# Where the inverse root of the RMS norms is made in a two-layer encoder trunk: sums land on all partitions by a tile of ones, logarithm and exponential in place of root, reciprocal and spread

## The chip, the core and the metric

One core of a Trainium2 chip runs the whole program. The metric is the device time in microseconds (us). The engines are called as in the profile: PE is TensorE (matmuls; PEld its weight loads), ACT is ScalarE, DVE is VectorE, POOL is GpSimd, and SP issues most DMAs.

## What is computed

A trunk of two layers on 512 tokens of width 1024, in float32. Each mixer and each feed-forward part stands between two RMS norms (from the reference):

```python
def rms_norm(x, g):
    y = xf * lax.rsqrt(jnp.mean(xf * xf, axis=-1, keepdims=True) + RMS_EPS) * g
for layer in range(DEPTH):
    h = rms_norm(x, norm_mix_pre[layer])
    m = even_mixer(h, ...) if layer % 2 == 0 else odd_mixer(h, positions, ...)
    x = x + rms_norm(m, norm_mix_post[layer])
    h = rms_norm(x, norm_ffn_pre[layer])
    f = conv_ffn(h, ...)
    x = x + rms_norm(f, norm_ffn_post[layer])
```

The even mixer is a gated linear recurrence beside stick-breaking attention, the odd one a sliding-window attention with rotary positions and sinks. The feed-forward part projects up to 2 x 2816, convolves over three tokens, gates, and projects down.

## The kernel before

**Layout.** Activations lie with the 1024 channels on partitions (8 tiles of 128) and the 512 tokens along the free axis, so a norm's sum runs over partitions. Each product of two float32 matrices is made of three matmuls (`three`, L1649): both factors are split into a high part, rounded to float32r, and a low part, the difference. ACT makes high parts (`split_hi`, L702; hx_hi), DVE low parts (`split_lo`, L1099; hx_lo). Weights come in units of 1 MB into a ring of three slots, loaded by SP.

**Norms before a matmul phase** (pre-norms p = 0 to 3). The gain is folded into hx_hi and hx_lo; the inverse root of a token, which is the same for all channels, is multiplied in when a result is taken out of PSUM, from the tile `rbc` (128 x 512, the same row on all partitions). ACT squares (`square`, L709), POOL (DVE for p = 0) adds up to `sumsq`. PE then makes token sums in columns (`mean_square`, L1705): for each 128 tokens a matmul with `sumsq` stationary and one column of ones moving. ACT takes the root (`root`, L717) into `std` (128 x 4), DVE the reciprocal `rcol` and four scaled identities `diag` (`inverse_rms`, L1120). PE multiplies `ones` with `diag`, which spreads the row over all partitions (`spread`, L1741), and DVE copies it to `rbc` (L1140). `rcol` itself is used as a column for the values of both attentions (L1287, L1042).

**Norms behind a phase** (boundaries bi = 0, 1, 2: the first mixer, the first feed-forward part, the second mixer). They go by token halves h = 0, 1, so that PE can begin with the next phase's half 0 while half 1 is being normed. `post_mean_square` (L1714) has one-column matmuls again, for two groups of tokens; in half 1 the last square is not added to `sumsq` but is a second source, which doubles them. `post_root` (L737), `post_inverse` (L1131) and `post_spread` (L1731) follow; the result stays in PSUM, in bank 6 or 7, left half. DVE then walks over the channel tiles (`boundary`, L1409): `normed` (L1421) the product into the right half of the bank, `add` (L1427) to x, `lo` (L1431) hx_lo, and ACT `hi` (L922) between. The last norm of all is made in another layout and has no part in this.

**Order.** Each engine has one queue, written out by hand; waits are semaphores. PE's places for the norm's matmuls are fixed steps in the stream of the projection: the sum of half 0 at step 4 and its spread at step 6 of the half 1 output (L1981 to L1986), those of half 1 at k = 5 and 7 of the next phase's first unit (`first_units`, L2011), the pre-norm's sum and spread as hooks within its third unit (L2034, L2037). `first_units` takes half 0 of two units, then half 1, each k behind `hx_ready`. In the second boundary ACT's queue is `raw(0)`, `root(2)`, then `raw(1)`; `raw` (L908) copies a query or key tile for the rotary, whose halves SP swaps by DMA (L550), 8 issues per tile, before DVE's products (`rope_finish`, L1548) and PE's first scores (`sw_scores`, L2117).

ACT needs the right function table. `preload_act_table_set` loads one ahead of its use; where a function is not in the loaded set, the compiler puts a load in front of it.

Of the kernel before, what the change touches and what calls it, by code (L numbers as in the profile page):

```python
# [21 lines left out]
P = 128  # L22
T = 512
# [129 lines left out]
def build(nc, io, out):  # L153
# [76 lines left out]
    diag = at("diag", [P, TT, P], F32, tmp0 + T * 4)  # L230
# [144 lines left out]

    def gate_bank(g):

        return bank(g % 3)
# [3 lines left out]
    def sb_set(h):  # L382
# [18 lines left out]
    sq_done, sum_done, ms_mm, std_done, rcol_done, diag_done, bc_mm, rbc_done = (sem(n) for n in (  # L401
        "sq_done", "sum_done", "ms_mm", "std_done", "rcol_done", "diag_done", "bc_mm", "rbc_done"))
    psq_done, psum_done, pms_mm, pstd_done, prcol_done, pdiag_done, pbc_mm = (sem(n) for n in (
        "psq_done", "psum_done", "pms_mm", "pstd_done", "prcol_done", "pdiag_done", "pbc_mm"))
# [231 lines left out]
    def _(pool):  # L636
# [12 lines left out]
        def whole_sums(bi, n):  # L649

            for i in range(1, n):
                pool.wait_ge(psq_done, post_squares(bi) + i + 1)
                if i == 1:
                    pool.wait_ge(ms_mm, bi + 1)
# [46 lines left out]
    def _(act):  # L701
# [52 lines left out]
        act.preload_act_table_set("sqrt_and_others")  # L754
# [17 lines left out]
        root(0)  # L772
# [145 lines left out]
        def boundary(bi, which, layer, last, splits):  # L918
# [6 lines left out]
            if bi == 1:  # L925
                act.preload_act_table_set("sqrt_and_others")
# [4 lines left out]
            post_root(bi, 0)  # L931
# [10 lines left out]
            post_root(bi, 1)  # L942
# [7 lines left out]
            root(bi + 1)  # L950

        def out_projection(layer):

            u = U_OUT[layer]
            act.preload_act_table_set("sqrt_and_others")
# [83 lines left out]
        act.wait_ge(unit_done, U_V + 1)  # L1039
        for t in range(TT):  # L1040
# [57 lines left out]
    def _(dve):  # L1098
# [21 lines left out]
        def inverse_rms(p):  # L1120

            dve.wait_ge(std_done, p + 1)
            if p:
                dve.wait_ge(pdiag_done, 2 * p)
            dve.reciprocal(rcol[:], std[:]).then_inc(rcol_done, 1)
            dve.wait_ge(rcol_done, p + 1)
            for t in range(TT):
                ins = dve.tensor_scalar(diag[:, t, :], ident, rcol[:, t:t + 1], None, ALU.mult)
            ins.then_inc(diag_done, 1)

        def post_inverse(bi, h):  # L1131

            dve.wait_ge(pstd_done, 2 * bi + h + 1)
            dve.reciprocal(rcol[:, 2 * h:2 * h + 2], std[:, 2 * h:2 * h + 2]).then_inc(prcol_done, 1)
            dve.wait_ge(prcol_done, 2 * bi + h + 1)
            for t in (2 * h, 2 * h + 1):
                ins = dve.tensor_scalar(diag[:, t, :], ident, rcol[:, t:t + 1], None, ALU.mult)
            ins.then_inc(pdiag_done, 1)

        def spread(p):  # L1140
            dve.wait_ge(bc_mm, p + 1)
            dve.tensor_copy(rbc[:], bank(6 if p else 4)).then_inc(rbc_done, 1)

# [48 lines left out]
        inverse_rms(0)  # L1192
        spread(0)
# [133 lines left out]
        for n in range(4):  # L1327
            evac(n)
        softplus_lambda()
        split_lo(3)  # L1330
        evac(4)
# [77 lines left out]
        def boundary(bi, post, pre, last, splits):  # L1409
# [238 lines left out]
    def _(pe):  # L1648
# [56 lines left out]
        def mean_square(p):  # L1705

            if p:
                pe.wait_ge(pstd_done, 2 * p)
            pe.wait_ge(sum_done, pre_sums(p + 1))
            for t in range(TT):  # L1710
                last = pe.matmul(bank(7)[:, t:t + 1], sumsq[:, P * t:P * t + P], ones[:, 0:1], start=t == 0, stop=t == TT - 1)
            last.then_inc(ms_mm, 1)

        def post_mean_square(bi, h):  # L1714

            if h:
                pe.wait_ge(pstd_done, 2 * bi + 1)
            else:
                pe.wait_ge(std_done, bi + 1)
# [3 lines left out]
            q = last_square(bi, h)  # L1723
            for t in (2 * h, 2 * h + 1):
                c = P * (t - 2 * h)
                srcs = (sumsq[:, P * t:P * t + P], sq[q % 3][:, HALF + c:HALF + c + P])[0:h + 1]
                for i, src in enumerate(srcs):
                    last = pe.matmul(bank(7)[:, t:t + 1], src, ones[:, 0:1], start=i == 0 and t == 2 * h, stop=i == h and t == 2 * h + 1)
            last.then_inc(pms_mm, 1)

# [577 lines left out]
```

## Time and profile before

| | us |
|---|---|
| median of 3 runs | 1085.07 (1084.81 to 1085.59) |
| the profiled execution | 1085.26 |
| its span, first to last instruction | 1083.5 |
| PE busy | 1074.3 |
| DVE busy | 688.2 |
| ACT busy | 478.2 |
| POOL busy | 59.2 |

### The profile page before, as it was taken

The page shows a single profiled execution, that of the slowest core. Times are in us where ns is not written, and L with a number is a line of the kernel's source. Part 1 is how long each engine was busy: PE and PEld are TensorE (multiplying, and loading weights), DVE is VectorE, ACT ScalarE, POOL GpSimd, SP SyncE. Part 2 cuts the span into 40 slices and gives each one's busy share as a digit, 9 for nine tenths or more (in the row PEclk, how much of TensorE's full clock was granted, in tenths as well). Part 3 has the DMA queues.
Part 4 walks back from the last instruction along what each step waited for, and adds up shares of the span by engine and source line. Part 5 has one row for each costly group of instructions (what it writes and reads, how often), then busy time and mean ns, then how long its engine had stood idle before and what let it go on. Part 6 is the DMA issues. An engine that isn't in the chain of part 4 may idle for free.

```text
span 1083.5 us, 14799 instructions
## 1 busy us (share of the span) xinstructions
PE 1074.3 (99%) x5860; PEld 906.6 (84%) x5860; DVE 688.2 (64%) x925; ACT 478.2 (44%) x691; POOL 59.2 (5%) x55
## 2 busy tenths in 40 slices
PE   9999999999999999999999999999999999999997
PEld 7876889988888888888899877998888888888886
DVE  6784975878767676522257877397867667751323
ACT  6455764645444444312235477464534343432321
POOL 0000002310000000001103000230000000000000
PEclk9999999999999999999999999999999999999999
DMA  7332141122222222232232513312323232321322
GB/s 237 117 117 75 45 153 67 52 79 106 90 103 90 96 97 93 92 107 82 94 118 68 181 59 117 117 40 79 117 78 116 77 116 77 117 78 61 114 97 77
DMA packets 23206, 105.61 MB, mean 97 GB/s; under 512 B 4080, under 2 KB 6896, under 8 KB 12528
## 3 DMA queue, kind: packets, MB, share of 16 engines
q1 hardware_dynamic: 23008, 104.84, 27.9%
q8 instruction: 39, 0.64, 0.2%
q14 instruction: 15, 0.12, 0.0%
q10 hardware_dynamic: 144, 0.01, 0.0%
HBM read 98.15 MB, written 2.10 MB: 93 GB/s over the span
## 4 chain that ended last, share of the span: by engine, by line
PE 93%; DVE 3%; ACT 2%; DMA 1%; issue 1%; SPq 0%; DVEq 0%
PE ps L1651 29%; PE ps L1653 29%; PE ps L1652 29%; PE ps L1835 1%; PE ps L1861 1%; PE ps L1846 1%; DVE ps L1421 1%; PE ps L2132 1%; DVE x L1427 1%; PE ps L2143 1%; DVE hx_lo L1431 1%; PE ps L2159 1%; ACT w_hi_s L707 1%; ACT prob L1056 0%; DVE w_lo_s L1103 0%
## 5 line engine op out<-in xcount | busy, mean ns | idle before, releaser
L1651 PE MATMUL ps<-hx_hi,w_hi 128*128 128x512 f32 x812 | 320.5, 395 | 0.3 <-DVE w_lo L1150 0.3
L1653 PE MATMUL ps<-hx_hi,w_lo 128*128 128x512 f32 x812 | 316.3, 390 | 0.0
L1652 PE MATMUL ps<-hx_lo,w_hi 128*128 128x512 f32 x812 | 316.2, 389 | 0.0
L1103 DVE TENSOR_TENSOR w_lo<-w_raw,w_hi 128x2048 fp32r<-128x2048 f32 (+1 forms) x74 | 167.6, 2265 | 119.5 <-ACT w_hi L707 119.4
L707 ACT ACTIVATE w_hi<-w_raw 128x2048 fp32r<-128x2048 f32 (+1 forms) x76 | 142.2, 1870 | 106.5 <-DMA w_raw<-in_ffn_w_down 90.8
L1651 PEld LDWEIGHTS ps<-hx_hi,w_hi 128*128 128x128 f32 x812 | 152.4, 188 | 37.7 <-issue 6.8
L1653 PEld LDWEIGHTS ps<-hx_hi,w_lo 128*128 128x128 f32 x812 | 152.4, 188 | 31.8
L1652 PEld LDWEIGHTS ps<-hx_lo,w_hi 128*128 128x128 f32 x812 | 152.5, 188 | 31.0 <-issue 0.5
L965 ACT ACTIVATE cg<-ug,vec 128x512 f32<-128x512 f32 x44 | 35.9, 816 | 140.8 <-DVE ug L1467 140.8
L1476 DVE SCALAR_TENSOR_TENSOR cg<-ug,vec,cg 128x511 f32<-128x511 f32 x88 | 65.8, 747 | 20.4 <-ACT cg L965 20.4
L977 ACT ACTIVATE g_hi<-cv 128x512 f32 (+1 forms) x44 | 27.8, 632 | 111.1 <-DVE cv L1485 111.1
L1467 DVE TENSOR_TENSOR ug<-ps,rbc 128x512 f32<-128x512 f32 x44 | 30.3, 690 | 61.4 <-PE ps L1653 61.4
L1651 PE MATMUL ps<-w_hi,g_hi 128*128 128x512 f32 x176 | 68.8, 391 | 0.0
L1653 PE MATMUL ps<-w_hi,g_lo 128*128 128x512 f32 x176 | 68.5, 389 | 0.0
L1652 PE MATMUL ps<-w_lo,g_hi 128*128 128x512 f32 x176 | 68.5, 389 | 0.0
L1476 DVE SCALAR_TENSOR_TENSOR cv<-uv,vec,cv 128x511 f32<-128x511 f32 x88 | 65.8, 747 | 0.0
L1487 DVE TENSOR_TENSOR g_lo<-cv,g_hi 128x512 f32 (+1 forms) x44 | 30.5, 692 | 37.0 <-ACT g_hi L977 37.0
L1651 PE MATMUL ps<-g_hi,w_hi 128*128 128x512 f32 x132 | 51.3, 389 | 0.0
L1652 PE MATMUL ps<-g_lo,w_hi 128*128 128x512 f32 x132 | 51.3, 389 | 0.0
L1653 PE MATMUL ps<-g_hi,w_lo 128*128 128x512 f32 x132 | 51.3, 389 | 0.0
L922 ACT ACTIVATE hx_hi<-x,vec 128x256 fp32r<-128x256 f32 x48 | 24.0, 506 | 34.1 <-DVE x L1427 34.0
L1653 PEld LDWEIGHTS ps<-w_hi,g_lo 128*128 128x128 f32 x176 | 33.0, 188 | 6.9
(260 smaller groups left out, 1878.0 us busy)
## 6 DMA issues: line engine op xcount, KB each, us to landing
w_raw<-in_ffn_w_up SPq DMA_DIRECT2D x40, 1024.0 KB, 4.8
w_raw<-in_ffn_w_down SPq DMA_DIRECT2D x16, 1024.0 KB, 4.9
w_raw<-in_even_w_in SPq DMA_DIRECT2D x6, 1024.0 KB, 4.9
w_raw<-in_even_w_out SPq DMA_DIRECT2D x3, 1024.0 KB, 4.8
w_raw_s<-in_odd_w_qkv SPq DMA_DIRECT2D x3, 1024.0 KB, 4.7
w_raw<-in_odd_w_qkv SPq DMA_DIRECT2D x3, 1024.0 KB, 5.1
w_raw<-in_odd_w_o SPq DMA_DIRECT2D x3, 1024.0 KB, 5.0
rsw<-rp SPq DMA_DIRECT2D x40, 64.0 KB, 2.0
```

Source lines behind the costliest of these rows:

```text
L707: act.activation(w_hi[buffer(u)][:, 0:k], w_raw[buffer(u)][:, 0:k], ACT.Copy).then_inc(w_hi_done, 1)
L922: act.activation(hx_hi[:, i, tokens_of(h)], x[:, i, tokens_of(h)], ACT.Identity, scale=gain(which, layer, i)).then_inc(hx_hi_done, 1)
L965: act.activation(cg[:], ug[:], ACT.Identity, scale=col(ffn_vec(layer, 2, j)), bias=col(ffn_vec(layer, 3, j))).then_inc(center, 1)
L977: act.activation(tile_(g_hi, j), cv[:], ACT.Copy).then_inc(g_hi_done, 1)
L1103: dve.tensor_tensor(w_lo[s][:, 0:k], w_raw[s][:, 0:k], w_hi[s][:, 0:k], ALU.subtract).then_inc(w_lo_done, 1)
L1421: dve.scalar_tensor_tensor(out=bank(6 + h)[:, HALF:T], in0=m[:, i, tokens_of(h)], scalar=gain(*post, i), in1=bank(6 + h)[:, 0:HALF], op0=A ...
L1467: dve.tensor_tensor(halves(ug[:]), out_tile(u, b0, 0), halves(rbc[:]), ALU.mult).then_inc(scaled, 1)
L1476: dve.scalar_tensor_tensor(out=dst[:, s:], in0=src[:, 0:T - s], scalar=col(ffn_vec(layer, 2 - s, j + FT * b)), in1=dst[:, s:], op0=ALU.mul ...
L1487: dve.tensor_tensor(tile_(g_lo, j), cv[:], tile_(g_hi, j), ALU.subtract).then_inc(g_ready, 1)
L1651: pe.matmul(dst, s_hi, r_hi, start=first, stop=False)
L1652: pe.matmul(dst, s_hi, r_lo, start=False, stop=False)
L1653: return pe.matmul(dst, s_lo, r_hi, start=False, stop=last)
```

## The change

The matmul that sums over partitions has `ones` (128 x 128) stationary and the squares moving. So every partition gets every token's sum at once, and no spread is needed. ACT makes the inverse root where it is wanted: `Ln` of (sum / 1024 + eps), then `Exp` of -0.5 times that. For the pre-norms this goes from the bank into `rbc`; for the boundaries it is in place in PSUM. DVE's reciprocals, scaled identities and copies are gone, and PE's spreads. For pre-norms 0 and 2, whose `rcol` is used, the four one-column matmuls stay (in a bank of their own), and ACT makes `rcol` by Ln and Exp too. The function set `sqrt_and_others` gives way to `natural_log_exp_and_others` around the norms; two preloads in the second layer go. The third boundary's half 0 sum now waits for the copy of the bank it overwrites, which its spread waited for. In the first half of a boundary DVE splits the weights of two units without a norm step between them.

```diff
-        def root(p):
+        def inverse_rms(p):
             act.wait_ge(ms_mm, p + 1)
-            act.activation(std[:], bank(7)[:, 0:TT], ACT.Sqrt, scale=1.0 / D, bias=eps).then_inc(std_done, 1)
+            act.activation(rbc[:], norm_bank(p), ACT.Ln, scale=1.0 / D, bias=eps).then_inc(log_done, 1)
+            act.wait_ge(log_done, p + 1)
+            act.activation(rbc[:], rbc[:], ACT.Exp, scale=-0.5).then_inc(rbc_done, 1)
+
+        def inverse_rms_columns(p):
+            act.wait_ge(col_mm, p // 2 + 1)
+            act.activation(std[:], norm_columns(p), ACT.Ln, scale=1.0 / D, bias=eps).then_inc(col_log, 1)
+            act.wait_ge(col_log, p // 2 + 1)
+            act.activation(rcol[:], std[:], ACT.Exp, scale=-0.5).then_inc(rcol_done, 1)
...
-        def post_root(bi, h):
+        def post_inverse(bi, h):
+            r = bank(6 + h)[:, 0:HALF]
             act.wait_ge(pms_mm, 2 * bi + h + 1)
-            act.activation(std[:, 2 * h:2 * h + 2], bank(7)[:, 2 * h:2 * h + 2], ACT.Sqrt, scale=1.0 / D, bias=eps).then_inc(pstd_done, 1)
+            act.activation(r, r, ACT.Ln, scale=1.0 / D, bias=eps).then_inc(plog_done, 1)
+            act.wait_ge(plog_done, 2 * bi + h + 1)
+            act.activation(r, r, ACT.Exp, scale=-0.5).then_inc(prms_done, 1)
...
             if bi == 1:
                 raw(0)
-            root(bi + 1)
+            inverse_rms(bi + 1)
+            if bi == 1:
+                inverse_rms_columns(2)
...
-            act.preload_act_table_set("sqrt_and_others")
+            if layer == 0:
+                act.preload_act_table_set("natural_log_exp_and_others")
...
-        act.preload_act_table_set("natural_log_exp_and_others")
         split_hi(U_QKV + 5)
...
-            post_inverse(bi, 0)
             for h in range(2):
-                dve.wait_ge(pbc_mm, 2 * bi + h + 1)
+                dve.wait_ge(prms_done, 2 * bi + h + 1)
...
-                if h == 0 and bi == 1:
-                    split_lo_part(splits[1], 0, UK // 2)
-                    post_inverse(bi, 1)
-                    split_lo_part(splits[1], UK // 2, UK)
-                elif h == 0:
-                    split_lo(splits[0])
-                    post_inverse(bi, 1)
+                if h == 0:
+                    if bi != 1:
+                        split_lo(splits[0])
                     split_lo(splits[1])
             split_lo(splits[2])
-            inverse_rms(bi + 1)
-            spread(bi + 1)
...
         def mean_square(p):
-            if p:
-                pe.wait_ge(pstd_done, 2 * p)
             pe.wait_ge(sum_done, pre_sums(p + 1))
-            for t in range(TT):
-                last = pe.matmul(bank(7)[:, t:t + 1], sumsq[:, P * t:P * t + P], ones[:, 0:1], start=t == 0, stop=t == TT - 1)
-            last.then_inc(ms_mm, 1)
+            pe.matmul(norm_bank(p), ones, sumsq[:], start=True, stop=True).then_inc(ms_mm, 1)
+            if p % 2 == 0:
+                for t in range(TT):
+                    last = pe.matmul(norm_columns(p)[:, t:t + 1], sumsq[:, P * t:P * t + P], ones[:, 0:1], start=t == 0, stop=t == TT - 1)
+                last.then_inc(col_mm, 1)
...
+            elif bi == 2:
+                pe.wait_ge(ahalf_evac, a_halves(2) + 3)
+            q = last_square(bi, h)
+            srcs = (sumsq[:, tokens_of(h)], sq[q % 3][:, HALF:T])[0:h + 1]
+            for i, src in enumerate(srcs):
+                last = pe.matmul(bank(6 + h)[:, 0:HALF], ones, src, start=i == 0, stop=i == h)
+            last.then_inc(pms_mm, 1)
```

## Rows read from the trace of the kernel before

**Rows 1.** The page, part 1: busy time of each engine
```profile
PE 1074.3 (99%) x5860; PEld 906.6 (84%) x5860; DVE 688.2 (64%) x925; ACT 478.2 (44%) x691; POOL 59.2 (5%) x55
```
**Rows 2.** The page, part 4: the chain that ended last, by engine
```profile
PE 93%; DVE 3%; ACT 2%; DMA 1%; issue 1%; SPq 0%; DVEq 0%
```
**Rows 3.** Waits of PE: engine, line, waited for: us in total, times, longest
```profile
PE ps L1651 <- DVE rp L1558: 0.7, 1, 0.7
...
PE ps L1738 <- DVE diag L1137: 0.2, 1, 0.2
```
**Rows 4.** Groups of PE: records, busy us, mean ns of one, idle before
```profile
L1711 PE MATMUL ps<-const,sumsq 128*128 128x1 f32 x32 | 3.8, 239 | 0.0
...
L1738 PE MATMUL ps<-diag,const 128*128 128x256 f32 x12 | 3.8, 395 | 0.2 <-DVE diag L1137 0.2
L1728 PE MATMUL ps<-const,sumsq 128*128 128x1 f32 x24 | 3.6, 235 | 0.0
```
**Rows 5.** Timeline of PE, first boundary, both halves: start, duration, what
```profile
184.94 0.50 PE L1728 MATMUL ps<-const,sumsq 128*128 128x1 f32 x4
...
185.50 0.28 PE L1652 MATMUL ps<-yb_lo,w_hi 128*128 128x256 f32 x1
...
186.80 0.59 PE L1738 MATMUL ps<-diag,const 128*128 128x256 f32 x2
...
187.35 0.28 PE L1652 MATMUL ps<-ya_lo,w_hi 128*128 128x256 f32 x1
...
201.14 0.28 PE L1653 MATMUL ps<-hx_hi,w_lo_x 128*128 128x256 f32 x1
201.40 0.35 PE L1728 MATMUL ps<-const,sumsq 128*128 128x1 f32 x2
...
202.48 0.28 PE L1652 MATMUL ps<-hx_lo,w_hi_x 128*128 128x256 f32 x1
```
**Rows 6.** Timeline of PE, pre-norm 1
```profile
222.54 0.95 PE L1711 MATMUL ps<-const,sumsq 128*128 128x1 f32 x8
...
223.67 0.39 PE L1652 MATMUL ps<-hx_lo,w_hi 128*128 128x512 f32 x1
```
**Rows 7.** Timeline of PE, second boundary, spread of half 1
```profile
568.78 0.28 PE L1653 MATMUL ps<-hx_hi,w_lo_s 128*128 128x256 f32 x1
569.14 0.70 PE L1738 MATMUL ps<-diag,const 128*128 128x256 f32 x2
```
**Rows 8.** Timelines of PE and DVE, third boundary, half 1
```profile
718.22 0.28 PE L1651 MATMUL ps<-hx_hi,w_hi_s 128*128 128x256 f32 x1
...
728.76 0.28 PE L1651 MATMUL ps<-hx_hi,w_hi_s 128*128 128x256 f32 x1
...
729.34 0.38 PE L1651 MATMUL ps<-hx_hi,w_hi_x 128*128 128x256 f32 x1
...
728.02 1.26 DVE L1431 SCALAR_TENSOR_TENSOR hx_lo<-x,vec,hx_hi 128x256 fp32r<-128x256 f32 x1
```
**Rows 9.** Timelines of ACT and DVE, first boundary, half 0
```profile
185.48 0.26 ACT L739 ACTIVATE std<-ps,narrow 128x2 f32<-128x2 f32 x1 [2.02 <-PE ps L1728]
...
187.43 0.49 DVE L1421 SCALAR_TENSOR_TENSOR ps<-m,vec,ps 128x256 f32<-128x256 f32 x1 [0.97 <-PE ps L1738]
```
**Rows 10.** Groups of ACT: activations out of PSUM, and one table load
```profile
L815 ACT ACTIVATE lru_r<-ps,vec 128x512 f32<-128x512 f32 x4 | 2.8, 688 | 3.9 <-PE ps L1877 3.9
...
L732 ACT ACTIVATE sq<-ps 128x256 f32<-128x256 f32 x6 | 2.3, 378 | 12.1 <-PE ps L1653 12.1
...
L775 ACT ACT_TABLE_LOAD x1 | 1.3, 1283 | 0.0
```
**Rows 11.** Timelines of ACT, SP's queue, DVE and PE, rotary of the second layer
```profile
589.33 1.08 ACT L915 ACTIVATE rp<-ps 128x512 f32<-128x512 f32 x2
...
587.46 10.51 SPq L556 DMA_DIRECT2D rsw<-rp  x16
...
609.70 1.28 DVE L1571 TENSOR_TENSOR qr<-rp,rsw 128x512 f32<-128x512 f32 x2
...
611.53 1.16 PE L2132 MATMUL ps<-kk,qr 64*128 64x64 f32 x16
```

More of the change, by code:

```diff
@@ L374, in half_bank, with norm_bank, norm_columns @@
         return n if n < 4 else 6 + n % 2
+    def norm_bank(p):
+        return bank(6 if p else 4)
+    def norm_columns(p):
+        return bank(7 if p else 5)[:, 0:TT]
     def gate_bank(g):
@@ L400, in build @@
         "hx_hi_done", "hx_ready", "post_t", "x_new", "m_first"))
[L401 to L404, printed above, removed]
+    sq_done, sum_done, ms_mm, col_mm, log_done, rbc_done, col_log, rcol_done = (sem(n) for n in (
+        "sq_done", "sum_done", "ms_mm", "col_mm", "log_done", "rbc_done", "col_log", "rcol_done"))
+    psq_done, psum_done, pms_mm, plog_done, prms_done = (sem(n) for n in (
+        "psq_done", "psum_done", "pms_mm", "plog_done", "prms_done"))
     ahalf_mm, ahalf_evac = sem("ahalf_mm"), sem("ahalf_evac")
@@ L653, in whole_sums @@
                 if i == 1:
-                    pool.wait_ge(ms_mm, bi + 1)
+                    if bi == 1:
+                        pool.wait_ge(ms_mm, bi + 1)
+                    else:
+                        pool.wait_ge(col_mm, bi // 2 + 1)
                     ins = pool.tensor_tensor(sumsq[:], sq[0][:], sq[1][:], ALU.add)
@@ L771, in _ @@
         split_hi(2)
-        root(0)
+        inverse_rms(0)
+        inverse_rms_columns(0)
         act.wait_ge(setup_v, 1)
@@ L925, in boundary @@
             if bi == 1:
-                act.preload_act_table_set("sqrt_and_others")
+                act.preload_act_table_set("natural_log_exp_and_others")
             for j, v in enumerate(last):
@@ L930, in boundary @@
                     split_hi(last[-1] + 1)
-            post_root(bi, 0)
+            post_inverse(bi, 0)
             if bi != 1:
@@ L941, in boundary @@
             split_hi(splits[1])
-            post_root(bi, 1)
+            post_inverse(bi, 1)
             for i in range(DT):
@@ L949, in boundary @@
                 raw(0)
-            root(bi + 1)
+            inverse_rms(bi + 1)
+            if bi == 1:
+                inverse_rms_columns(2)
         def out_projection(layer):
             u = U_OUT[layer]
-            act.preload_act_table_set("sqrt_and_others")
+            if layer == 0:
+                act.preload_act_table_set("natural_log_exp_and_others")
             whole_squares(2 * layer, 0, u)
@@ L1039, in _ @@
         act.wait_ge(unit_done, U_V + 1)
+        act.wait_ge(rcol_done, 2)
         for t in range(TT):
@@ L1118, in split_columns @@
                 dve.tensor_tensor(w_lo[s][:, :, b], w_raw[s][:, :, b], w_hi[s][:, :, b], ALU.subtract).then_inc(done, 1)
-        def inverse_rms(p):
-            dve.wait_ge(std_done, p + 1)
-            if p:
-                dve.wait_ge(pdiag_done, 2 * p)
-            dve.reciprocal(rcol[:], std[:]).then_inc(rcol_done, 1)
-            dve.wait_ge(rcol_done, p + 1)
-            for t in range(TT):
[L1128 to L1142, printed above, removed]
         dve.memset(narrow[:, 9, 0:1], EPS)
@@ L1191, in _ @@
         split_lo(2)
-        inverse_rms(0)
-        spread(0)
         chain = sem("setup_chain")
@@ L1327, in _ @@
         for n in range(4):
+            if n == 3:
+                dve.wait_ge(col_mm, 1)
             evac(n)
@@ L1330, in _ @@
         split_lo(3)
+        dve.wait_ge(rcol_done, 1)
         evac(4)
@@ L1722, in post_mean_square @@
                 pe.wait_ge(psq_last, 2 * bi + 2)
[L1723 to L1729, printed above, removed]
-        def post_spread(bi, h):
-            pe.wait_ge(pdiag_done, 2 * bi + h + 1)
-            if h:
-                pe.wait_ge(pstd_done, 2 * bi + 2)
             elif bi == 2:
                 pe.wait_ge(ahalf_evac, a_halves(2) + 3)
-            pe.matmul(bank(6 + h)[:, 0:HALF], ones, diag[:, 2 * h:2 * h + 2, :].rearrange("p t c -> p (t c)"),
-                      start=True, stop=True).then_inc(pbc_mm, 1)
-        def spread(n):
-            pe.wait_ge(diag_done, n + 1)
-            pe.matmul(bank(6 if n else 4), ones, diag[:].rearrange("p t c -> p (t c)"), start=True, stop=True).then_inc(bc_mm, 1)
+            q = last_square(bi, h)
[3 more added lines that the diff above has]
+            last.then_inc(pms_mm, 1)
         def first_step():
@@ L1828, in sb_z @@
                 pe.wait_ge(yb_ready, p)
+            if p == 0:
+                pe.wait_ge(rcol_done, 1)
             if p == 2:
@@ L1933, in first_norm @@
                 mean_square(0)
-            if n == 9:
-                spread(0)
         half(4, first_norm)
@@ L1984, in out_halves @@
                             post_mean_square(bi, 0)
-                        if h and step == 6:
-                            post_spread(bi, 0)
                         step += 1
@@ L2002, in down_halves @@
                             post_mean_square(1, 0)
-                        if h and k == 6:
-                            post_spread(1, 0)
                         last = down_half(u, h, k, k0)
@@ L2019, in first_units @@
                         post_mean_square(bi, 1)
-                    if j == 0 and k == 7:
-                        post_spread(bi, 1)
                     pe.wait_ge(hx_ready, DT + 2 * DT * bi + k + 1)
@@ L2034, in first_units @@
                 tokens(u + 2, group_banks(group_of(u + 2)),
-                       {(0, 2): lambda: mean_square(2), (1, 4): lambda: spread(2)}).then_inc(unit_done, 1)
+                       {(0, 2): lambda: mean_square(2)}).then_inc(unit_done, 1)
             else:
-                unit(u + 2, hx, hooks={(0, 1): lambda: mean_square(bi + 1), (0, 6): lambda: spread(bi + 1)})
+                unit(u + 2, hx, hooks={(0, 1): lambda: mean_square(bi + 1)})
         def ffn(layer, bi):
```

9 lines of the change are left out of this document (removed).

## The prediction

> **What bounds the kernel.** I read the page's busy shares first: TensorE is at work in 99% of the span [rows 1]. The chain that ended last is 93% PE [rows 2]. The waits of PE then say how much of the rest lies in the middle: beside the start-up the longest is 0.7 us, behind a rotary product, and one of 0.2 us lies at a spread, L1738 [rows 3]. So the time is the sum of PE's own instructions: whatever is taken off PE's stream shortens the kernel, as long as the other engines keep up at the places where they already nearly don't. ScalarE is busy 44% and VectorE 64%, and work moved between them is worth something only there.
>
> **The state of things at a norm.** There are ten norm steps: four before a matmul phase (p = 0 to 3, all tokens) and six after one (three boundaries, two token halves). Each does a matmul group with one moving column, a root on ScalarE, a reciprocal and scaled identities on VectorE, and a second matmul that spreads the result. In the groups every float32 matmul shows as two records: 32 of L1711 for the four pre-norms, 24 of L1728 on the running sums of the six post-norms, 12 of L1738 for six spreads [rows 4]. L1728 has 12 more by the code, where half 1 reads the last square as a second source: four per boundary.
>
> **Part 1, PE's stream.** I price each insertion by start to start: from the start of the inserted group to the start of the second ordinary matmul behind it, less the one ordinary pitch that would be there anyway. (The first one behind still shows the inserted group's tail.) The ordinary pitch is 0.12 us at 256 columns and 0.23 at 512.
> - Half 0 of a boundary: the four one-column records start at 184.94 and the second matmul behind at 185.50 [rows 5]: 0.56 - 0.12 = 0.44 us. The spread starts at 186.80, the second behind at 187.35: 0.55 - 0.12 = 0.43. Before: 0.87. After: one 256-column matmul of float32 with `ones` stationary. It has the shape of the spread, so 0.43. Saved 0.44, three times: 1.32.
> - Half 1: eight one-column records, from 201.40 to 202.48 [rows 5]: 1.08 - 0.12 = 0.96. With the spread 1.39. After: two 256-column matmuls, 0.86. Saved 0.53, three times: 1.59.
> - Pre-norms 1 and 3: eight one-column records, 222.54 to 223.67 [rows 6]: 1.13 - 0.23 = 0.90; the 512-column spread is replaced by a 512-column matmul with the same cost. Saved 0.90 twice: 1.80.
> - Pre-norms 0 and 2 keep the one-column group for `rcol`, and swap the spread one for one: 0.
>
> The sum is 4.7 us. As a check by count: 52 one-column records go (36 of L1728, 16 of the 32 of L1711), at 0.90 / 8 = 0.11 each 5.8 us, and three 256-column matmuls come, 1.3 us: 4.5.
>
> The rows show 0.11 us for a record with a single column. The Trainium skill, "TensorE: Matmul & The Clock Gate", section "Back-to-back issue gap", speaks against a gain of this size: it gives a matmul of 1 to 64 columns only an issue floor of about 62 ns. By that floor, as an estimate, the 52 records would return 3.2 us and the sum would be 1.9. I stay with the rows, because they are these instructions at these places, each with its own weight load.
>
> **Part 2, small waits of PE.** A spread had to wait for VectorE, or PE for hx_lo. In the first boundary PE pauses 0.15 us ahead of the half 1 group (201.14 + 0.11 to 201.40) [rows 5]; in the second 0.25 us ahead of the spread (568.78 + 0.11 to 569.14) [rows 7]; in the third 0.24 us at 729.34 (728.76 and three pitches of 0.113, to 729.10), right when the hx_lo that starts at 728.02 ends, 729.28 [rows 8]. The spread's wait goes with the spread. The other two go if VectorE's chain moves forward by more than PE does.
> That chain now: group at 184.94, root at 185.48, reciprocal, two scaled identities, spread on PE at 186.80, first VectorE product at 187.43 [rows 5, 9]: 2.49 us. After: matmul 0.59 (as the spread's record [rows 5]), Ln and Exp over 128x256 in PSUM, two hand-overs. No row has a Ln. From below, a 256-column activation out of PSUM takes 0.38 (L732); from above, a 512-column one with a bias tile takes 0.69 (L815) [rows 10]. I take 0.45 for Ln, near the end of its own width, and 0.38 for Exp; with 0.05 per hand-over and 0.05 to VectorE about 1.6 us. So the chain starts 0.9 us earlier, against 0.44 that PE gained. From both bounds: 0.9 + 0.07 to 0.9 - 0.55 us. In half 1 VectorE also loses the reciprocal and the identities from its own queue. They lie between the root's end, 185.74, and the spread, 186.80, so they take at most 1.1 us; I take 0.5. That makes 1.4 us earlier in all, against PE's 1.1 to 1.2. The 0.64 us of waits go: total 5.3.
>
> **Part 3, at no cost, and what covers it.** ScalarE gets longer work: Ln and Exp of 512 columns instead of a 4-column root, some 1.1 us more at each pre-norm, 0.6 at each half. It idles 2.02 us ahead of the root in rows 9. VectorE loses the copy into rbc (and the reciprocals and identities), so rbc is there sooner: PE had no wait for it, so that gives nothing. Three table loads of 1.28 us go (L775 [rows 10], and the ones of the second output projection and behind the value copies); ScalarE waits there, so nothing. New waits: post half 0 of the third boundary waits for the m copy two steps earlier than now; the other waits are for results that are produced before or together with the sums.
> The tight one is pre-norm 2. ScalarE's queue there is raw(0), root, raw(1), and raw(1) feeds SP, which swaps halves by DMA for the rotary. Four activations instead of one, behind a longer matmul pair, start raw(1) about 1.6 us later (matmul 0.86 more, Ln 0.69, Exp 0.6, two tiny ones, less the root and the idle): its end goes from 590.41 [rows 11] to 592.0. SP issues 16 swaps back to back in 10.51 us from 587.46, so the ninth, the first that needs raw(1), starts at 592.7. Cover 2.3 us, need 1.6. If that cover were gone, 1 us late here is 1 us late at the scores: the rotary product ends at 610.98 and PE starts the scores at 611.53 [rows 11].
>
> **The forecast.** The profiled execution took 1085.26 us; less 5.3 is 1080.0. It stands 0.19 above the median of the runs, 1085.07; from that, **1079.8 us**. A change of 0.2% is 2.2 us, about what a measurement of this kernel can tell from none.
> Its own range is 1078.0 to 1081.5: the ordinary 256-column pitch is 0.118 in one stretch (185.50 to 186.80, eleven matmuls [rows 5]) and 0.113 in another (718.22 to 728.76, 93 of them [rows 8]). Over some 150 matmuls behind each spread that is 0.7 us, and nothing in the rows says what decides it: it may flip for the better at two boundaries, or for the worse at the third. The waits may stay (+0.6).
>
> **Rivals.**
> 1. *VectorE's chain becomes the bound of the boundaries.* For it: the third boundary already waits for hx_lo [rows 8]. Against it: VectorE gets less work and an earlier start. If Ln and Exp together take 0.7 longer than I put them, VectorE moves by less than PE: the third boundary gives back up to 1.1, the first up to 0.8, and the 0.4 of hx_lo and sum waits stay. 5.3 - 2.3 = 3.0: 1082.1. Chance 0.16.
> 2. *The rotary chain starts late.* raw(1) later than its cover by 1 to 2 us: PE stands still as long before the first scores. 1079.8 + 1.5 = 1081.3. Decides from 2.3 us of delay. Chance 0.06.
> 3. *One-column records cost less than their pitch.* Part of their 0.11 us [rows 4, 6] may be a refill of the queue that the float32 matmul in their place pays too. At half of it, 52 x 0.055 = 2.9 us of the 4.7 don't come: 4.7 - 2.9 + 0.64 = 2.4, 1082.7. Against it: the spreads, priced the same way, show no such refill, 0.43 for two records. Chance 0.05. By the issue floor of the Trainium skill, cited above, it would come out near this.
> 4. *Slower: Ln and Exp do not stay in one loaded table.* Then each pair brings two more loads of 1.28 [rows 10] into the chain: 2.6 us more per half, so VectorE starts 1.7 later than now, and PE reaches it 1.1 earlier. With what VectorE saves in half 1 that is a stall of 2.3 us at a boundary, in two of them 4.6. At pre-norm 2 four loads add 5.1 to the 1.6, against 2.3 of cover: 4.4. 4.6 + 4.4 - 4.7 = 4.3 slower: 1089.4. It decides from one extra load per activation. Chance 0.04. The Trainium skill, "ScalarE: Activation LUTs", section "Table sets: the hidden batching unit", speaks against this rival: it lists exp and ln in one set. This kernel names that set, but no row shows a Ln in it.
> 5. *Next to nothing*, by several of these together: 0.04.
>
> The forecast has 0.65. Faster by over 0.2%: 0.65 + 0.16 + 0.06 + 0.04 of rival 3 = 0.91; same 0.05, slower 0.04. The range is 1078.0 to 1083.0: it takes in rivals 1 to 3 and leaves out about 0.15.
>
> **What would show it.** Right: no L1738 or L1744, one-column records only at pre-norms 0 and 2 (16); PE's busy time lower by 4 to 5 us; first VectorE product of a boundary about 1.6 us behind the matmul; no waits of PE at the three places; ACT_TABLE_LOAD 12 instead of 15. Wrong: a wait of PE on hx_lo (L1431) of over 0.3 us (rival 1), one at the first scores (rival 2), a PE time that falls by only 2 (rival 3), table loads at each norm (rival 4).

## The result and the profile after

The kernel after takes **1079.51 us** (median of 5 runs, 1078.30 to 1080.07) against 1084.96 (1084.81 to 1085.59) before, measured beside it. The ratio is 0.9946, 95% interval 0.9935 to 0.9958: 5.5 us less. The prediction said 1079.8, between 1078.0 and 1083.0. The profiled execution of after took 1078.84 us, its span is 1077.1; that of before had 1083.5, so the pair of profiles differs by 6.4 us, 1 us more than the medians.

The page, part 1, and the chain that ended last, by engine (as [rows 1, 2]):
```profile
PE 1067.2 (99%) x5814; PEld 899.7 (84%) x5814; DVE 678.8 (63%) x882; ACT 482.7 (45%) x702; POOL 58.8 (5%) x55
...
PE 94%; DVE 3%; ACT 1%; DMA 1%; SPq 1%; issue 0%; DVEq 0%; ACTq 0%
```
TensorE is as much the bound as it was. Its busy time fell by 7.1 us, to the same share. It has 46 records fewer: 52 with one column gone, 6 with 256 columns more (three products of two records).

The waits of PE (as [rows 3]; the first two lines are start-up, before 12 us, the second of them 0.3 us in the first profile of before and 1.1 in a second one):
```profile
PE ps L1762 <- DVE warm L1149: 1.2, 1, 1.2
PE ps L1649 <- DVE w_lo L1154: 0.9, 2, 0.7
PE ps L1649 <- DVE w_lo_s L1131: 0.5, 1, 0.5
PE ps L1649 <- issue: 0.5, 1, 0.5
```
The waits for `diag` and for `rp` are gone. The last two lines are new, and lie in the second boundary.

Groups of PE and ACT in the kernel after (as [rows 4, 10]):
```profile
L1706 PE MATMUL ps<-sumsq,const 128*128 128x512 f32 x8 | 4.1, 592 | 0.0
L1722 PE MATMUL ps<-sumsq,const 128*128 128x256 f32 x12 | 3.6, 378 | 0.0
L1709 PE MATMUL ps<-const,sumsq 128*128 128x1 f32 x16 | 1.9, 240 | 0.0
...
L730 ACT ACTIVATE rbc<-ps,narrow 128x512 f32<-128x512 f32 x4 | 2.8, 688 | 19.0 <-PE ps L1706 19.0
L761 ACT ACTIVATE ps<-ps,narrow 128x256 f32<-128x256 f32 x6 | 2.7, 448 | 8.0 <-PE ps L1722 8.0
...
L763 ACT ACTIVATE ps<-ps 128x256 f32<-128x256 f32 x6 | 2.2, 368 | 0.2
```
L761 is the logarithm of a half, 448 ns, L763 its exponential, 368 ns. The prediction had put 0.45 and 0.38. There is no table load in between: 12 loads in all, as forecast.

Timelines of PE, ACT and DVE in the first boundary of the kernel after (as [rows 5, 9]):
```profile
184.60 0.59 PE L1722 MATMUL ps<-sumsq,const 128*128 128x256 f32 x2
...
185.15 0.28 PE L1650 MATMUL ps<-yb_lo,w_hi 128*128 128x256 f32 x1
...
200.47 0.59 PE L1722 MATMUL ps<-sumsq,const 128*128 128x256 f32 x2
200.90 0.59 PE L1722 MATMUL ps<-sq,const 128*128 128x256 f32 x2
...
201.45 0.28 PE L1650 MATMUL ps<-hx_lo,w_hi_x 128*128 128x256 f32 x1
...
185.23 0.45 ACT L761 ACTIVATE ps<-ps,narrow 128x256 f32<-128x256 f32 x1 [2.00 <-PE ps L1722]
185.71 0.37 ACT L763 ACTIVATE ps<-ps 128x256 f32<-128x256 f32 x1
...
186.11 0.49 DVE L1426 SCALAR_TENSOR_TENSOR ps<-m,vec,ps 128x256 f32<-128x256 f32 x1 [4.10 <-ACT ps L763]
```
By the prediction's way of pricing, half 0 costs PE 185.15 - 184.60 - 0.12 = 0.43 us and half 1 201.45 - 200.47 - 0.12 = 0.86. Both are the figures of the prediction. From the product to VectorE's first step it is 186.11 - 184.60 = 1.51 us, where it was 2.49 and 1.6 was estimated.

**Where the 6.4 us of the pair lie.** I set the two PE streams beside each other, matmul by matmul: each ordinary matmul starts some time earlier in after than in before, and the table says where that lead grows and by how much. Boundary 1 is the first boundary, bi = 0.

| place | forecast | measured |
|---|---|---|
| half 0 of the boundaries 1, 2, 3 | 0.44 each | 0.47, 0.48, 0.43 |
| half 1 of boundary 1, with its wait | 0.53 + 0.15 | 0.64 |
| half 1 of boundary 2, with its wait | 0.53 + 0.25 | 0.81 |
| half 1 of boundary 3 | 0.53 | 0.95 |
| hx_lo at the end of boundary 3 | 0.24 | 0.10 |
| pre-norms 1, 3 | 0.90 each | 0.91, 0.91 |
| pre-norms 0, 2 | 0 | 0, 0 |
| sum of these | 5.3 | 5.7 |
| pitch of unchanged 256-column matmuls, three stretches | (range only) | +0.5, +0.4, +0.5 |
| new waits at 560.37 and 584.00 | 0 | -0.5, -0.6 |
| a rotary wait near 660, start-up, rest | 0 | +0.8, -0.2, -0.2 |

The last three lines are no part of the forecast sum. Whether they belong to the change is what some of the experiments ask.

The first new wait, in the timelines of ACT, DVE and PE in the second boundary of the kernel after:
```profile
555.23 1.92 ACT L717 ACTIVATE w_hi_s<-w_raw_s 128x2048 fp32r<-128x2048 f32 x1 [0.46 <-DMA w_raw_s<-in_odd_w_qkv]
...
557.58 0.49 DVE L1436 SCALAR_TENSOR_TENSOR hx_lo<-x,vec,hx_hi 128x256 fp32r<-128x256 f32 x1 [0.85 <-ACT hx_hi L947]
557.98 2.28 DVE L1131 TENSOR_TENSOR w_lo_s<-w_raw_s,w_hi_s 128x2048 fp32r<-128x2048 f32 x1
...
560.37 0.36 PE L1649 MATMUL ps<-hx_hi,w_hi_s 128*128 128x256 f32 x1 [0.47 <-issue]
...
584.00 0.35 PE L1649 MATMUL ps<-w_hi_s,hx_hi 128*128 128x256 f32 x1 [0.53 <-DVE w_lo_s L1131]
```
and the same two splits on VectorE in the kernel before:
```profile
560.72 2.29 DVE L1103 TENSOR_TENSOR w_lo_s<-w_raw_s,w_hi_s 128x2048 fp32r<-128x2048 f32 x1
...
583.88 3.38 DVE L1103 TENSOR_TENSOR w_lo_s<-w_raw_s,w_hi_s 128x2048 fp32r<-128x2048 f32 x1
```
In after ScalarE waits for the weights of the second layer's first unit, its hx_hi comes behind that split, VectorE idles 0.85 us for the hx_hi, and its own split ends at 560.26. PE starts 0.11 later ("issue" in that row hides whose end it is; the end of the split shows it). In before the split ended at 563.01 and PE started at 563.11, after only 0.15 us of standing. So this hand-over was tight already. The split moved forward by 2.75 us, but PE came 3.2 us sooner, since its pitch (the time from one matmul's start to the next) had become faster behind the sum at 547. The same at the second place: the split ends 3.40 us sooner (583.86 for 587.26), PE would have been there 4.0 sooner. The gain of pitch in this boundary (0.4 + 0.5) and the new waits (0.5 + 0.6) are one thing: what PE gains behind the point where the others take their start, it gives back at the next hand-over.

### The profile page after: what moved, and what is told of

Same layout as the page of the kernel before. It is cut to its first block, busy times and chain, and to the rows that moved or that the text cites. A ratio compares the mean times of both kernels' runs of the same rounds, so it can differ in the third digit from the quotient of the medians.

```text
span 1077.1 us, 14667 instructions
## 1 busy us (share of the span) xinstructions
PE 1067.2 (99%) x5814; PEld 899.7 (84%) x5814; DVE 678.8 (63%) x882; ACT 482.7 (45%) x702; POOL 58.8 (5%) x55
## 4 chain that ended last, share of the span: by engine, by line
PE 94%; DVE 3%; ACT 1%; DMA 1%; SPq 1%; issue 0%; DVEq 0%; ACTq 0%
PE ps L1649 30%; PE ps L1651 29%; PE ps L1650 29%; PE ps L1814 1%; PE ps L1840 1%; PE ps L1825 1%; DVE w_lo_s L1131 1%; PE ps L2103 1%; PE ps L2114 1%; DVE hx_lo L1436 1%; PE ps L2130 1%; ACT prob L1084 0%; DMA w_raw<-in_even_w_in 0%; DMA w_raw_s<-in_odd_w_qkv 0%; PE ps L1856 0%
## 5 line engine op out<-in xcount | busy, mean ns | idle before, releaser
L1131 DVE TENSOR_TENSOR w_lo_s<-w_raw_s,w_hi_s 128x2048 fp32r<-128x2048 f32 (+1 forms) x10 | 24.0, 2398 | 25.2 <-ACT w_hi_s L717 25.2
```

Source lines behind the costliest of these rows:

```text
L1131: dve.tensor_tensor(w_lo[s][:, 0:k], w_raw[s][:, 0:k], w_hi[s][:, 0:k], ALU.subtract).then_inc(w_lo_done, 1)
```

## The experiments

All times are medians; each kernel was timed beside the kernel before, whose runs lay between 1084.2 and 1085.9. A change of a few tenths of a microsecond is below what these medians tell; there the profile is read.

### The one-column products put back

```diff
+            for t in (2 * h, 2 * h + 1):
+                c = P * (t - 2 * h)
+                cols = (sumsq[:, P * t:P * t + P], sq[q % 3][:, HALF + c:HALF + c + P])[0:h + 1]
+                for i, src in enumerate(cols):
+                    pe.matmul(bank(6 + h)[:, HALF + t:HALF + t + 1], src, ones[:, 0:1], ...)
             srcs = (sumsq[:, tokens_of(h)], sq[q % 3][:, HALF:T])[0:h + 1]
```
and the four products of a pre-norm, into bank 7, at p = 1 and 3 too.

> The kernel after, with the 52 one-column records that the change removed put back on TensorE, their results read by nobody: 36 ahead of the post-norm sums and 16 at the pre-norms 1 and 3. Theory (the time came from TensorE's stream, at 0.11 us a record): 52 x 0.11 = 5.7 us more than the kernel after, 1079.5 + 5.7 = 1085.2, and the same waits of TensorE as after. Rival 3 (a one-column record costs well under the pitch, half of it in its version of 1082.7): 2.9 us or less, 1082.4. If the gain were from the shorter chain on ScalarE and VectorE, next to nothing: 1079.5 to 1080.2.

Measured: **1085.85 us** (11 runs, 1084.91 to 1087.32), ratio to before 1.0008 (0.9999 to 1.0017). It is 6.3 us above after, where 5.7 was expected. The distance between its PE stream and that of after grows by 0.50, 0.89, 0.90, 0.48, 0.85, 0.43, 0.89 and 0.95 at the eight places, 5.9 in all, or 0.113 us for each of the 52 records. The groups:
```profile
PE 1073.8 (99%) x5866; PEld 907.0 (84%) x5866; DVE 678.6 (63%) x882; ACT 482.7 (45%) x702; POOL 58.7 (5%) x55
...
L1727 PE MATMUL ps<-const,sumsq 128*128 128x1 f32 x24 | 3.4, 229 | 0.0
...
PE ps L1649 <- DVE rp L1556: 0.6, 1, 0.6
```
PE's busy time is 6.6 us up and 52 records came back, while VectorE and ScalarE stand within 0.2 us of after. That the waits would be those of after was expected and did not come out: one for `rp` (0.6 us, in the fence) is back, and the one at the second split is gone.
The other side: this kernel has the new, shorter chain in full. It also has six records more than before, the three more products of 256 columns, 1.3 us by the prices above, and it is 0.8 us slower than before (1085.02 beside it). So the shorter chain and the waits give back some 0.5 us at most, of the size of the 0.64 of Part 2, and the interval of the ratio, 2 us wide, does not tell that from nothing.

### A longer chain on ScalarE: one and three more pairs

```diff
             act.activation(r, r, ACT.Ln, scale=1.0 / D, bias=eps).then_inc(plog_done, 1)
-            act.wait_ge(plog_done, 2 * bi + h + 1)
+            for k in range(2):
+                act.wait_ge(plog_done, 3 * (2 * bi + h) + k + 1)
+                act.activation(r, r, ACT.Ln if k % 2 else ACT.Exp).then_inc(plog_done, 1)
+            act.wait_ge(plog_done, 3 * (2 * bi + h + 1))
             act.activation(r, r, ACT.Exp, scale=-0.5).then_inc(prms_done, 1)
```
The second kernel has `range(6)` and 7 in place of 3.

> One more pair (exponential, logarithm) between the logarithm and the exponential of each half of a post-norm, 0.45 + 0.37 = 0.82 us later for VectorE's first product, six times. By the slack read in the profile after: first boundary 2.0 us at the last k of half 1, so nothing; second boundary none at two places (the waits at 560.37 and 584.00), 0.8 us, and up to 0.8 more; third boundary 0.2 us at the last k of half 1, so 0.6 us. Theory: 1.4 to 2.2 us more than after, 1080.9 to 1081.7. Rival 1 (VectorE's chain is the bound at each half): 6 x 0.82 = 4.9 us, 1084.4. Chain wholly covered: 1079.5.

> Three more pairs in each half of a post-norm, 3 x 0.82 = 2.5 us. By the same slacks: first boundary 2.5 - 2.0 = 0.5 us; second boundary 2.5 us, and up to 2.5 more in half 1; third boundary 2.5 - 0.2 = 2.3 us. Theory: 5.3 to 7.8 us more than after, 1084.8 to 1087.3, more than three times what one pair costs. Rival 1: 6 x 2.5 = 15 us, 1094.5.

Measured: **1080.46 us** with one pair (1079.43 to 1081.29), 0.95 above after; **1087.68** with three (9 runs, 1086.88 to 1089.42), 8.2 above. One pair cost less than the 1.4 to 2.2 us expected: the wait at 584.00 did not grow, the one at 560.37 by 0.2 us. Three cost more than the 5.3 to 7.8. So 0.8 us a half cost about 1 us over six halves, and the next 1.6 us a half cost 7. Rival 1 in its strong form would have been 4.9 and 15. The slack is real nearly everywhere, and it is short.

The waits of PE with three pairs, and the timelines of ACT, POOL and PE in its third boundary:
```profile
PE ps L1652 <- issue: 2.3, 1, 2.3
PE ps L1725 <- POOL sumsq L685: 1.7, 1, 1.7
PE ps L1652 <- DVE w_lo_s L1134: 1.5, 1, 1.5
...
716.27 0.36 ACT L752 ACTIVATE sq<-ps 128x256 f32<-128x256 f32 x1
...
716.71 0.75 POOL L685 TENSOR_TENSOR sumsq<-sumsq,sq 128x256 f32<-128x256 f32 x1 [1.15 <-ACT sq L752]
...
717.52 0.70 PE L1725 MATMUL ps<-sumsq,const 128*128 128x256 f32 x2 [1.66 <-POOL sumsq L685]
```
The first and third lines are the two splits of the second boundary, as expected. The second line is one that neither theory named. It costs more than hx_lo, the wait that I had looked for in the third boundary (1.0 us in three waits). In ScalarE's queue the squares of half 1 stand behind the hx_hi of half 0, each of which waits for VectorE. A late inverse root of half 0 delays those squares, POOL's last sum, and so the sum of half 1 on PE. In after that last sum ends at 709.28 and PE takes it at 709.90: 0.6 us of slack. The stream of PE loses 1.9 us to after there.

A second cost lies in the second boundary and is no wait. Behind the wait of 2.30 us at 562.77 the granted clock of TensorE is 0.50, its lower level of 1.2 GHz, for 3.4 us, and then 1.00 again. PE's matmuls and the clock (PEclk) of that stretch:
```profile
562.77 0.55 PE L1652 MATMUL ps<-hx_hi,w_hi_s 128*128 128x256 f32 x1 [2.30 <-issue]
...
564.19 0.42 PE L1652 MATMUL ps<-hx_hi,w_hi_s 128*128 128x256 f32 x1
...
core 0: us, PE busy (x) PEld busy (x) DVE busy (x) ACT busy (x) POOL busy (x), PEclk, DMA share, GB/s
562.80:566.10 3.30, 3.30 (x15) 3.30 (x16) 1.57 (x4) 2.54 (x5) 0.76 (x1) 0.50 0.52 218
```
The pitch is 0.213 us in place of 0.113, and the distance to after grows by 1.5 us over these sixteen matmuls. In after, whose longest waits behind the start-up are 0.5 us, the clock stays at 1.00 up to 1076.3, behind the last matmul. These two, the sum behind POOL and the clock, are what the expectation of 5.3 to 7.8 us did not have in it.

### Two table loads to each pair

```diff
             act.wait_ge(plog_done, 2 * bi + h + 1)
+            act.preload_act_table_set("natural_log_exp_and_others")
             act.activation(r, r, ACT.Exp, scale=-0.5).then_inc(prms_done, 1)
+            act.preload_act_table_set("natural_log_exp_and_others")
```
and the same at the pre-norms, one of them in the columns' pair.

> A load of the function set between the logarithm and the exponential of each pair, and one more behind the exponential, as if the two functions lay in different sets (2 x 1.283 us a pair, 12 pairs with those of the columns). Rival 4 of the prediction put this at some 1089.4, 9.6 us more than forecast, all of it on the path. By the slacks: first boundary 0 to 0.6 us, second 1.3 to 3.9, third 1.1 to 2.4, the pre-norms 0 to 1.3 each for the wait for the spread at their end: theory 3 to 8 us more than after, 1082.5 to 1087.5.

Measured: **1085.76 us** (11 runs, 1084.85 to 1087.71), ratio 1.0009 (1.0000 to 1.0018), 6.2 above after. So rival 4 would have taken the gain and left a draw, not a kernel slower by 4.3 us. PE's distance to after grows by 0.7 at 561, by 1.5 and 0.5 at the rotary, and by 3.8 at the sum of half 1 in the third boundary: 2.1 for the same wait behind POOL as above (1.93 us, at 715.16), and 1.7 behind it, where the granted clock is 0.50 from 715.52 to 718.93 and the pitch 0.213 us. The mean clock of the runs, 0.997 or 0.998 in nine of eleven, suggests that it fell in most of them; the two at 1.000 took 1085.48 and 1086.13, no less than the others, so what the fall is worth in the median stays open. ScalarE and SP's queue there, in this kernel, and PE's wait:
```profile
587.68 1.28 ACT L732 ACT_TABLE_LOAD   x1
...
592.61 1.07 ACT L945 ACTIVATE rp<-ps 128x512 f32<-128x512 f32 x2
...
584.97 13.19 SPq L563 DMA_DIRECT2D rsw<-rp  x16
...
PE ps L1654 <- DVE rp L1559: 1.2, 1, 1.2
```
and in the kernel after:
```profile
587.49 1.07 ACT L940 ACTIVATE rp<-ps 128x512 f32<-128x512 f32 x2
...
583.45 10.10 SPq L563 DMA_DIRECT2D rsw<-rp  x16
```
In after, raw(1) ends 588.56 - 583.45 = 5.1 us behind the first swap, and eight swaps take 5.05: the cover is just used up and nothing is lost (the 16 swaps go out in 10.10 us, in before in 10.51 [rows 11]). With the loads it ends 8.7 us behind and the swaps stretch to 13.19, 3.1 longer. Of that, 1.5 and 0.5 us reach PE. This is rival 2, brought about on purpose: here about two thirds of the stretch are paid, first at a PSUM bank that the rotary must free and only then at the scores.

### Both kernels once more, for what varies

Unchanged copies of after and of before.

> The kernel after, unchanged, on the chip of the next three. Its five runs lay between 1078.30 and 1080.07, 1.8 us apart; those of before 0.8. Two of the gains in the profile have no cause in the change: a wait of 0.7 us for rp at 656 that was gone (SP issued the eight swaps ahead of it in 4.94 us instead of 5.85), and a drift of 0.4 to 0.5 us in three stretches where 256-column matmuls went at 0.113 us instead of 0.118. If both vary from run to run, the median here is again 1079 to 1080.5 and the profile may show the wait or the slower pitch; if they belong to the kernel, the wait is gone again and the drift stands.

> The kernel before, unchanged, for a second profile. If the wait of 0.7 us for rp near 656 and the pitch of 0.118 us from 165 to 185 and from 552 to 560 belong to the kernel, both are here again; if they vary from run to run, one or both are missing, and the 0.8 and 0.5 us that the first pair of profiles puts there are no part of the change's gain. The time: 1084.2 to 1085.9.

Measured: after again 1079.65 (1079.35 to 1080.05); before again 1085.3, one run. Between the first and second profile of before PE ends within 0.03 us, but the parts moved: the drift from 160 to 183 is there between them (its pitch now 0.113 us there too), the wait for rp is shorter, and a wait of 0.64 us at the first scores (611.92) is new. Waits of PE and SP's queue in the second profile of before, and SP's queue in the first:
```profile
PE ps L1651 <- DVE rp L1558: 0.3, 1, 0.3
...
652.82 5.44 SPq L556 DMA_DIRECT2D rsw<-rp  x8
```
```profile
652.42 5.85 SPq L556 DMA_DIRECT2D rsw<-rp  x8
```
In both profiles of after the same eight took 4.94 and PE has no wait for rp; with the columns put back it was 5.71 and 0.6. So the 0.8 us at 660 in the first pair go with how fast SP issued eight DMAs, and their size varies from run to run. But the wait is in both profiles of before and in neither of after, so whether 0.3 us or more of it belong to the change is open. The 0.5 us of drift in the first boundary come from the run. So does a wait of 0.52 us for `probT` at 662.58 in the second profile of after, which the first doesn't have. The drift from 552 to 584 stands: the mean pitch from 550 to 560 and from 570 to 580 is 0.1173 to 0.1179 us in both profiles of before, 0.1133 or 0.1134 in both of after. The two new waits stand in both of after as well, 0.7 and 0.5 us in the second. By this pair of second profiles the difference is 5.85 us, nearer to the 5.5 of the medians. The places of the forecast, summed in the same way, give 5.7 in this pair as in the first: what varies is the rest.

### One record for each product with the ones

```diff
+    ones_r = place("ones_r", [P, P], F32R)
...
-    sumsq = place("sumsq", [P, T], F32)
+    sumsq = place("sumsq", [P, T], F32R)
...
-            pe.matmul(norm_bank(p), ones, sumsq[:], start=True, stop=True).then_inc(ms_mm, 1)
+            pe.matmul(norm_bank(p), ones_r[:], sumsq[:], start=True, stop=True).then_inc(ms_mm, 1)
...
-            srcs = (sumsq[:, tokens_of(h)], sq[q % 3][:, HALF:T])[0:h + 1]
+            srcs = (sumsq[:, tokens_of(h)], sq_r[q % 3][:, HALF:T])[0:h + 1]
...
-                last = pe.matmul(bank(6 + h)[:, 0:HALF], ones, src, start=i == 0, stop=i == h)
+                last = pe.matmul(bank(6 + h)[:, 0:HALF], ones_r[:], src, start=i == 0, stop=i == h)
```
`sq_r` names the same bytes as `sq` in the other type. The running sums are rounded to that type each time they are written.

> The squares' sums and the tile of ones in the type of the kernel's other products, so that each product with the ones is one record at the pitch of 0.11 us for 256 columns and 0.22 for 512, in place of two at 0.43 and 0.86 us together; the one-column products stay as they are. Theory (TensorE's stream is the bound): 9 x (0.43 - 0.11) = 2.9 us and 4 x (0.86 - 0.22) = 2.6 us, 5.4 us less than after, 1074.1, less whatever of it turns into waits at the places without slack (0.5 to 1 us in the second boundary): 1074 to 1075. If the waits take it all back: 1078 or more. Each sum is also handed on 0.3 to 0.6 us sooner.

Measured: **1075.73 us** (1074.62 to 1076.48), ratio to before 0.9917 (0.9903 to 0.9930): 3.8 us under after and 9.2 under before, the fastest of all. The groups of PE, with the page's first line ahead, and its waits:
```profile
PE 1062.1 (99%) x5801; PEld 896.5 (84%) x5801; DVE 679.0 (63%) x883; ACT 482.6 (45%) x702; POOL 58.8 (5%) x55
...
L1727 PE MATMUL ps<-sumsq,ones_r 128*128 128x256 f32 x6 | 1.7, 280 | 0.0
L1711 PE MATMUL ps<-sumsq,ones_r 128*128 128x512 f32 x4 | 1.6, 394 | 0.0
...
PE ps L1654 <- DVE w_lo_s L1135: 1.1, 2, 0.6
PE ps L1654 <- issue: 0.7, 1, 0.7
...
PE ps L1654 <- DVE hx_lo L1441: 0.4, 1, 0.4
```
At the places of the products the streams part by 0.30 to 0.32 us for each one of 256 columns and 0.62 to 0.64 for one of 512, all as expected. Then 0.3 us go at 558, 0.6 at 564.5 and 0.6 in the last half of the third boundary: VectorE's splits and hx_lo. That is the mechanism of rival 1, met 4 us further on instead of at the change itself: 5.4 taken off PE gave 3.8, and the 1074 to 1075 expected were missed.

### The splits moved

```diff
                 for i in range(DT):
-                    lo(h, i)
                     if i == 5 and h == 0 and bi == 1:
                         split_lo(splits[0])
+                    lo(h, i)
+                    if i == 5 and h == 1 and bi == 1:
+                        split_lo_part(splits[2], 0, UK // 2)
```
and the other half of that split where the whole one was.

> The kernel after with two splits moved in VectorE's order in the second boundary alone: that of the first unit one place earlier, ahead of a wait of 0.85 us for ScalarE, and half of that of the third unit ahead of the last two residues. Theory (both new waits of TensorE are for these splits, 0.49 us at 560.37 and 0.62 at 584.00): 0.4 to 1.1 us less than after, 1078.4 to 1079.1. Rival (the weights of the first unit come in too late for any order, and the half split delays the last residues): 0 to 0.6 us, or slower by 0.3.

> The one-record sums and the moved splits together. Theory (TensorE reaches the second boundary 3 us sooner than after, so that the splits matter more): 1073.0 to 1074.0, at least 0.5 us under the one-record kernel alone. If the moved splits do nothing: the same as the one-record kernel.

Measured: **1079.38 us** alone (1079.03 to 1080.94) and **1075.60** with the one-record products (1075.39 to 1076.33): the same as without the moves, 1079.6 and 1075.7. The theories had put 1078.4 to 1079.1 and 1073.0 to 1074.0: both missed. Waits of PE with the moves alone:
```profile
PE ps L1654 <- DVE hx_lo L1436: 0.6, 1, 0.6
...
PE ps L1654 <- DVE w_lo_s L1131: 0.3, 1, 0.3
```
Against after, PE gained 0.52 us at 560 and 0.65 at 584, as the theory had it. It lost 0.39 at 566.9, where the next split now ended later, and 0.79 at 580.6, where hx_lo stood behind the half split. So the second half of the rival holds (the half split delays the last residues), and the first does not: an earlier place did help the first unit. The order moves the wait and doesn't remove it.

## Why the prediction was right

- **Part 1, PE's stream: right in mechanism and size.** The forecast was 4.7 us from start to start; putting the 52 records back costs 5.9 of PE's stream by the profiles, less 1.3 for the three new products makes 4.6, and the way of counting records (5.8 - 1.3 = 4.5) gives it too. Half 0, half 1 (with its wait) and the pre-norms each came within 0.04 us, but for half 1 of the third boundary.
- **Part 2, the small waits: the sum right, one place wrong, and that by luck.** The waits of boundaries 1 and 2 went. Of the 0.24 us for hx_lo in the third boundary only 0.10 came back: after still waits there, a few matmuls earlier. VectorE moved forward hardly more than PE did, as rival 1 had it for that place. What made up for it is a wait ahead of the third boundary's spread, which the prediction didn't read: 0.33 us in before (from 716.55 to 716.99, less one pitch of 0.11). That is most of the 0.95 in place of 0.53. That the two errors nearly cancel is luck.
- **The chain from the sum to VectorE: right.** 1.51 us against 1.6, the logarithm 0.448 against 0.45, the exponential 0.368 against 0.38.
- **New waits: missed.** The prediction looked for rival 1 at hx_lo, and it came at the weight splits of the second boundary, 1.1 us of it. The rows that would have told were the ends of those splits in before, 0.1 us ahead of PE at 563. It cost nothing in the total, because it took back 0.9 us of faster pitch that the prediction hadn't in its sum either. The total agrees for the forecast's reasons in its 5.7 us of places; that what lay outside them came to little is luck. The hoped-for end of the range (a better pitch at two boundaries, down to 1078.0) did not come: the better pitch of the second boundary was given back.
- **Part 3, raw(1): right that it costs nothing, the delay too small.** It starts 4.0 us behind the first swap where it was 1.9, so 2.2 us later; 1.6 was forecast, 2.3 covered. The price of the work was right: from the sum's start on PE to raw(1) it is 587.49 - 584.78 = 2.71 us, where it was 1.15. The other 0.6 is the new wait at 584.00, which lies between raw(0) and the sum. So the missed wait all but used up this cover as well.
- **Rivals.** 1 is false at its size, 2.3 us given back; a part of it, in the second boundary, was there, and it comes true a little further on (three pairs, one-record products). 2 has its mechanism but not its case. 3 is false. 4 is false, and its price was too high: 6.2 us measured, 9.6 put, though the price had no fall of the clock in it; I had taken each load as paid in full at two boundaries and the whole excess at the rotary.
- **The table set.** L761 and L763 follow each other at 0.03 us with no load. Here the trace agrees with the Trainium skill, "ScalarE: Activation LUTs", section "Table sets: the hidden batching unit", cited in rival 4.

What stays open: what puts the stream of 256-column matmuls at 0.113 or 0.118 us. The pitch changes at a norm's products or at a wait: in after it falls to 0.113 right behind the sum at 547.03, in both profiles, and in before not until 563. With the one-record products it stays at 0.118 until the wait at 558. No run tells what decides it.

## What to carry to other kernels

When one engine is busy 99% of the span, price a change by the start-to-start time of the instructions that it takes from that engine, and count products of one column as full ones. Then, for every other engine, write down the slack at each hand-over behind the change, the weight splits and the sums of the next half among them: here it was from 0.1 to some 2 us, so a gain of 5.5 us passed and the next 5.4 gave 3.8. Look at the granted clock behind every long wait: here waits of 2.30 and 1.93 us were each followed by 3.4 us at half the clock. And take second profiles before a difference of half a microsecond is given a cause.

## What was not expected of the hardware

- A float32 product with a single moving column took two records of 0.11 us, 0.226 us in all, more than half of what one with 256 columns took (0.43). The same 256 columns in the type of the other products cost 0.11 to 0.12.
- The granted clock of TensorE fell in the middle of two profiled executions, for 3.4 us each, right behind PE's waits of 2.30 us (562.77, three pairs) and 1.93 us (715.16, two loads), and cost 1.5 and 1.7 us. In the other nine no wait behind the start-up is longer than 0.95 us, and the clock stays at 1.00 to the end of the stream. With three pairs two more waits, of 1.50 and 1.66 us, had no fall behind them.
- The ordinary matmul of 256 columns has two pitches, 0.1133 and 0.1178 us, both in stretches whose granted clock is 1.00, and each holds for tens of microseconds: a difference of 0.5 us in each such stretch.
- SP issued the same eight swaps in 4.94, 5.44 or 5.85 us, 5.71 in the kernel with the columns put back, which sets when the rotary product frees PE's bank.
- hx_lo of 256 columns on VectorE takes 0.48 us, but often 1.2 to 1.6 where POOL sums 512 columns at the same time, and a split 3.38 where it takes 2.28:
```profile
569.82 1.56 DVE L1436 SCALAR_TENSOR_TENSOR hx_lo<-x,vec,hx_hi 128x256 fp32r<-128x256 f32 x1
...
580.48 3.38 DVE L1131 TENSOR_TENSOR w_lo_s<-w_raw_s,w_hi_s 128x2048 fp32r<-128x2048 f32 x1
...
576.10 5.60 POOL L653 TENSOR_TENSOR sumsq<-sumsq,sq 128x512 f32<-128x512 f32 x4 [1.43 <-ACT sq L725]
```
These rows are of the kernel after. The long split is in before too (3.38 us at 583.88), so the change didn't make it; it is the one ahead of the second new wait. A split that began before POOL's sum (527.36, POOL from 527.88) took 2.29 us, and there POOL's two sums took 4.35 us together where one alone takes 1.30. No run here takes the sums off POOL, so what that would give is open.
